# Token rows of the expert dispatch in their own order of channels, loaded into TensorE with a stride of eight columns

## The reference

```python
h2 = modln(x, g_ffn[l], sh_f, sc_f)            # rmsnorm(x, g) * (1 + scale) + shift
# hier_moe: a group by argmax, then the best two experts inside it
xd = zeros((nb * MOE_BLK, d)).at[dest].set(xt[t_s])      # token rows gathered by expert
hid = silu(xb @ w_g[e]) * (xb @ w_u[e])                  # 1024 -> 256, for each expert
yd = hid @ w_d[e]                                        # 256 -> 1024
y = zeros((n, d)).at[t_s].add(yd[dest] * w_s[:, None])
```

## Time and profile before

| | |
|---|---|
| median of three runs | 1427.52 us (1427.38 to 1430.2) |
| the profiled execution, its own time | 1426.45 us |
| its span in the trace | 1424.6 us |
| TensorE busy, mean granted clock | 1215.2 us (85%), 0.945 of full |
| weight loads busy | 919.1 us |
| VectorE / ScalarE busy | 632.7 us / 455.8 us |
| DMA | 356.03 MB, mean 250 GB/s |

### The profile page before, as it was taken

One profiled execution on the slowest core, in us unless ns is written; L12 is line 12 of the kernel. 1 busy time (PEld: TensorE's weight loads), 2 busy tenths in 40 slices (PEclk: granted clock), 3 DMA queues, 4 the chain that ended last, 5 costly groups with the idle time before them and its releaser, 6 DMA issues.

```text
span 1424.6 us, 22233 instructions
## 1 busy us (share of the span) xinstructions
PE 1215.2 (85%) x8870; PEld 919.1 (65%) x8870; DVE 632.7 (44%) x1445; ACT 455.8 (32%) x1043; POOL 138.5 (10%) x175
## 2 busy tenths in 40 slices
PE   5999887999998959999988379998998588888871
PEld 3788754888888647556665278857998464555540
DVE  1545686455445592222221374586767621121213
ACT  2533466433343420001000374265665200010002
POOL 1510000111103230000000200000102000000001
PEclk9999999999999969999999679999999799999996
DMA  9952245323323578999999683267564479999994
GB/s 350 321 168 75 74 152 185 109 89 98 110 89 123 204 260 316 411 419 418 420 422 411 230 243 125 83 205 225 179 186 141 161 323 423 421 420 423 417 422 145
DMA packets 128927, 356.03 MB, mean 250 GB/s; under 512 B 20456, under 2 KB 82144, under 8 KB 104256
## 3 DMA queue, kind: packets, MB, share of 16 engines
q1 hardware_dynamic: 116560, 317.68, 59.5%
q0 software_dynamic: 6528, 18.59, 4.4%
q10 hardware_dynamic: 5744, 18.43, 3.3%
HBM read 332.62 MB, written 22.06 MB: 249 GB/s over the span
## 4 chain that ended last, share of the span: by engine, by line
PE 70%; DMA 12%; DVE 10%; issue 4%; ACT 3%; SPq 0%; POOL 0%; DVEq 0%; ACTq 0%; POOLq 0%
PE banks L924 32%; PE banks L1153 12%; PE banks L1167 7%; DMA ring<-in_w_e_down 6%; PE banks L1145 5%; PE banks L1092 4%; DMA ring<-in_w_e_up 3%; PE banks L1020 2%; PE banks L864 2%; PE banks L1035 2%; PE banks L1005 2%; DMA ring<-in_w_mod 1%; DMA ring<-in_w_in 1%; PE banks L1117 1%; DMA att<-expert_rows,slots_u 1%
## 5 line engine op out<-in xcount | busy, mean ns | idle before, releaser
L1795 DVE TENSOR_TENSOR w_lo<-ring,w_hi 128x256 fp32r<-128x256 f32 x480 | 222.8, 474 | 240.6 <-ACT w_hi L1429 239.4
L1429 ACT ACTIVATE w_hi<-ring 128x256 fp32r<-128x256 f32 x480 | 197.4, 416 | 303.0 <-PE banks L924 253.9
L1153 PE MATMUL banks<-ring,arena 128*64 128x256 f32 x2048 | 233.3, 383 | 33.1 <-issue 16.9
L924 PE MATMUL banks<-h_hi,w_hi 128*128 128x512 f32 (+1 forms) x640 | 221.3, 346 | 7.0 <-DVE h_lo L1726 5.8
L1153 PEld LDWEIGHTS banks<-ring,arena 128*64 128x64 f32 x2048 | 157.0, 137 | 100.3 <-issue 30.6
L924 PE MATMUL banks<-h_lo,w_hi 128*128 128x512 f32 (+1 forms) x640 | 219.8, 343 | 0.0
L924 PE MATMUL banks<-h_hi,w_lo 128*128 128x512 f32 (+1 forms) x640 | 219.6, 343 | 0.0
L1167 PE MATMUL banks<-ring,att 128*64 128x512 f32 x512 | 123.6, 626 | 25.9 <-issue 15.8
L924 PEld LDWEIGHTS banks<-h_hi,w_hi 128*128 128x128 f32 x640 | 122.4, 191 | 23.8 <-ACT arena L1400 5.2
L924 PEld LDWEIGHTS banks<-h_lo,w_hi 128*128 128x128 f32 x640 | 122.5, 191 | 13.7
L924 PEld LDWEIGHTS banks<-h_hi,w_lo 128*128 128x128 f32 x640 | 122.3, 191 | 13.9
(11 more groups left out here) (219 smaller groups left out, 1510.2 us busy)
## 6 DMA issues: line engine op xcount, KB each, us to landing
ring<-in_w_e_gate SPq DMA_DIRECT2D x64, 1024.0 KB, 9.0
ring<-in_w_e_up SPq DMA_DIRECT2D x64, 1024.0 KB, 9.8
ring<-in_w_e_down SPq DMA_DIRECT2D x64, 1024.0 KB, 10.0
ring<-in_w_mod SPq DMA_DIRECT2D x48, 1024.0 KB, 5.2
ring<-in_w_in SPq DMA_DIRECT2D x38, 1024.0 KB, 6.0
expert_rows<-arena ACTq DMA_DIRECT2D x32, 512.0 KB, 8.3
ring<-in_w_o SPq DMA_DIRECT2D x8, 1024.0 KB, 5.1
ring<-in_w_branch SPq DMA_DIRECT2D x8, 640.0 KB, 4.9
```

Source lines behind the costliest of these rows:

```text
L924: ins = mm(out_ap, a, b, start=k == 0 and p_ == 0, stop=k == KD - 1 and p_ == 2)
L1153: ins = mm(banks[e * CAP:(e + 1) * CAP, bank, 0:DE], x[:, k, e * CAP:(e + 1) * CAP], w[:, k * DE:(k + 1) * DE], start=k == 0, stop=k == KD ...
L1429: fn(w_hi[:, u % AHEAD, :, :], chunk(key)[:, q * KU:(q + 1) * KU, :], ACT.Copy).then_inc(w_hi_ready, 1)
L1795: v.tensor_tensor(w_lo[:, u % AHEAD, :, :], chunk(key)[:, q * KU:(q + 1) * KU, :], w_hi[:, u % AHEAD, :, :].bitcast(F32), ALU.subtract).th ...
```

## The change

The row stays in its own order everywhere. Both layers write `htok` plainly, the passes for hi and lo are contiguous in both layers, `turn_h` in layer 1 reads `k::KD`, as layer 0 does already, and `pick_x` loads `h[:, tt, k::KD]` as weights: 128 columns of four bytes, 32 bytes from one to the next. The number of instructions on every engine, their sizes, their order and their waits stay as they were.

```diff
-                        rows = htok[:, tt, k * P:(k + 1) * P] if l else htok[:, tt, k::KD]
+                        rows = htok[:, tt, k::KD]
...
-                        ins = mm(out, h[:, tt, k * P:(k + 1) * P], picked[:, tt, :],
+                        ins = mm(out, h[:, tt, k::KD], picked[:, tt, :],
                                  start=tt == 0 and h is th_hi, stop=tt == QT[l] - 1 and h is th_lo)
...
-                    if l:
-                        ins = fn(htok[:, tt, :].rearrange("p (k s) -> p k s", k=KD)[:, :, 64:P],
-                                 X[:, tt, 512:D].rearrange("p (s k) -> p k s", k=KD), ACT.Copy, scale=r)
-                    else:
-                        ins = fn(htok[:, tt, 512:D], X[:, tt, 512:D], ACT.Copy, scale=r)
-                    ins.then_inc(f_x_act, 1)
+                    fn(htok[:, tt, 512:D], X[:, tt, 512:D], ACT.Copy, scale=r).then_inc(f_x_act, 1)
...
-                        fn(th_hi[:, tt, :].rearrange("p (k s) -> p k s", k=KD),
-                           htok[:, tt, :].rearrange("p (s k) -> p k s", k=KD), ACT.Copy).then_inc(th_hi_ready, 1)
+                        fn(th_hi[:, tt, :], htok[:, tt, :], ACT.Copy).then_inc(th_hi_ready, 1)
...
-                    if l:
-                        ins = v.tensor_scalar(htok[:, tt, :].rearrange("p (k s) -> p k s", k=KD)[:, :, 0:64],
-                                              X[:, tt, 0:512].rearrange("p (s k) -> p k s", k=KD), r, None, ALU.mult)
-                    else:
-                        ins = v.tensor_scalar(htok[:, tt, 0:512], X[:, tt, 0:512], r, None, ALU.mult)
-                    ins.then_inc(f_x_dve, 1)
+                    v.tensor_scalar(htok[:, tt, 0:512], X[:, tt, 0:512], r, None, ALU.mult).then_inc(f_x_dve, 1)
...
-                    h = htok[:, tt, :]
-                    hi, lo = th_hi[:, tt, :], th_lo[:, tt, :]
-                    if l == 0:
-                        h = h.rearrange("p (s k) -> p k s", k=KD)
-                        hi, lo = (x.rearrange("p (k s) -> p k s", k=KD) for x in (hi, lo))
-                    v.tensor_tensor(lo, h, hi.bitcast(F32), ALU.subtract).then_inc(th_lo_ready, 1)
+                    v.tensor_tensor(th_lo[:, tt, :], htok[:, tt, :], th_hi[:, tt, :].bitcast(F32), ALU.subtract)\
+                        .then_inc(th_lo_ready, 1)
```

## The result

The changed kernel takes 1483.31 us, the median of four runs (1479.52 to 1486.01), against 1428.86 us for the kernel before on the same chip (1427.38 to 1433.63): a ratio of 1.037, 95% interval 1.0344 to 1.0396. It is slower, as forecast, but by 54 us and not by 35, and outside the range.

What follows compares the result with a forecast made beforehand. Transfers were taken to bound the expert-stage quads, TensorE close behind. Terms -3.7 + 4.1 + 37 - 4 + 1.7 = +35.1 us on 1426.45 gave 1461.5, forecast 1462 us with the runs' median; range 1423 to 1470.

Steps and rivals of the forecast that it cites:

- the price of a load: Dispatch: the stride halves the load rate, 107 to 213 ns, +107 ns per load at full clock, starts 226 ns apart.
- The savings: Plain row passes: 3.2 us before layer 0's first dispatch, 0.5 us in layer 1, 3.7 us in all.
- The bound of +120: Dispatch: upper bound per load, from L888's 30 ns more for each 32 columns; total then 1469 us.
- L888's pace: Strided loads of `modr` columns: 128, four side by side, in 2.11 us, 66 ns for each four.
- rival 2: Dispatch: load longer by 52 ns as in transposes, pace near 171 ns, +8.6 us, 1436 us; chance 0.14 including values between.
- At half clock a load of 213 ns still fits: Layer 0, quad 0: 26 of 64 matmuls run at half clock and pay nothing for the stride.
- the two quads 0: First quad of each layer, not covered by transfers: +4.1 us in layer 0, +1.7 us in layer 1.
- Layer 0's seven quads: Expert stage: TensorE becomes the bound at 37.7 us a quad, 264 instead of 227.1 us, +37.
- Rival 1: Dispatch: the strided load is hidden, starts stay at 119 ns, only savings remain, 1423.8 us; chance 0.24.
- With the transfers ahead of TensorE these 5 us mostly go: Layer 0's last two pairs, without dispatch: weight waits and a matmul stretch from a clock fall mostly vanish, -4 us.
- Hidden behind the transfers: Layer 1's other quads: 3.4 us added makes 30.9, below the transfers' 32.2 us, so nothing lost.
- layer 1 loses its cover as well: Rival 3: layer 1's quads no longer hidden, up to 24 us more, 1470 to 1486 us; chance 0.02.

Runs made afterwards that it cites:

- the spread order: Changed kernel with each quad's dispatch spread evenly over two pairs, two parts in each, strided loads kept: 1473.59 us against 1429.81 for the kernel before, ratio 1.0297.
- its counterpart: Kernel before with the dispatch spread evenly over two pairs in the same way, loads contiguous: 1426.7 us against 1429.81, ratio 0.9981.

## Why the prediction was right, and where it was wrong

The direction was right, and so was what bounds layer 0 afterwards; the size was not: 53 us by the spans where 35 were forecast. Three steps of the working failed. The largest is the cover in layer 1, put at nothing lost and measured at 11.0 us; then the price of a load, 107 ns taken and 122 measured; then the waits of the last pairs of layer 0, which did not go (-4 forecast, +0.4 measured).

**The savings: right.** L1773 (L1789 before) takes 4.63 us, forecast 4.62; ACT's passes 1057 ns, forecast near 1.06 us; the idle time 10.64 us, forecast 10.6; and it passed whole to TensorE, -3.4 us. The run with contiguous loads agrees with the sum, -4.6 against -3.7 us. The -3.9 us between the stages are more than the row passes of layer 1 (-0.5): there the transposes of L878 met the full clock in the profiled run and the half clock in that of before (16 in 3.65 us, now 2.03), and so did L1117 (4.71, now 3.64 us). That comes to 2.7 us and is a matter of when the clock rises, not of the edit: with the edit too the 16 transposes took 3.65 us in the run with the spread order, and without it 3.07 in its counterpart.

**The price of a load: right in kind, too small.** Forecast +107 ns and starts of 226 ns; measured +122 and 241. The load's own row was to be near 295 ns and is 337: it grew by 149 ns, more than the starts moved apart. The bound of +120, which I worked out from L888's 30 ns for 32 columns and did not take, was right to 2 ns. So was L888's pace: all but the passage of the last, (2.11 - 0.14) / 32 = 62 ns for 32 columns, is 1.9 ns a column and 246 ns for 128. I set it aside as four readers of one memory and took "double", which fits both kinds of strided load loosely and the dispatch's own kind not best. The transposes' loads (192 against 140 ns for the same 128 lines) follow another price, and why is open; leaning on them was the mistake behind rival 2.

**"At half clock a load of 213 ns still fits": wrong in size.** The load costs 241 ns at either level of the clock, so it adds 28 ns to 213 there too. With 28 and 122 ns in place of 0 and 107 the two quads 0 come to +5.4 and +2.4 us; measured +5.0 and +2.0, forecast 4.1 and 1.7.

**Layer 0's seven quads: right.** TensorE became the bound, DMA share 0.89 (under 0.9 forecast), 268.3 us against 264. By the form of my own sum, 30.9 + 64 x 0.122 = 38.7 us a quad, 271 for seven; measured 38.2 and 268.3. Rival 1 fell with the first load.

**"With the transfers ahead of TensorE these 5 us mostly go": wrong.** The last pairs of layer 0 in the changed kernel, as in the earlier trace rows:

```profile
816.41 3.67 PE L1153 MATMUL banks<-ring,arena 128*64 128x256 f32 x32 [0.94 <-issue]
822.24 3.67 PE L1153 MATMUL banks<-ring,arena 128*64 128x256 f32 x32 [2.16 <-issue]
828.25 3.65 PE L1167 MATMUL banks<-ring,att 128*64 128x512 f32 x16 [2.33 <-issue]
```

The waits are there as before. The clock did not fall this time (granted 1.00 from 814 to 823 us, where it was 0.68 from 779.6 to 785.0 before), so the second row takes 3.67 us and not 5.36, but the down product then waits 2.33 us where it waited 0.17: the weights set its time. The ring has six slots, the chunks of one pair; a transfer can be ahead by that and no more, however long TensorE was the bound before. Six chunks of 1 MB take 15 us at 421 GB/s, and a pair without dispatch takes TensorE 11.4 us: it runs dry inside the pair.

**"Hidden behind the transfers" in layer 1: wrong, and the largest miss (11.0 us).** I compared means over a quad, 30.9 against 32.2 us. But the dispatch of a quad stands wholly in one of its two pairs. By the hidden transposes, the pairs of layer 1 took 16.0 and 16.1 us before, and take 20.8 and 12.9 after. In the long one TensorE is behind and gives its slots back late; in the short one TensorE catches up with 11.4 us of work, and 15 us of transfers can't follow, so it waits for weights: 0.4 to 0.6 us in five of the seven short pairs and, more, 1.4 to 2.5 us in five of the seven long ones, for chunks that were issued in the short pair before. Three such pairs of the changed kernel, short, long, short, by windows; then SyncE's and TensorE's timelines around the change from short to long; then the waits of SyncE's queue over the seven quads (us in all, times, longest):

```profile
1244.30:1256.67 12.37, 11.09 (x83) 5.75 (x82) 3.33 (x9) 0.39 (x1) 0.00 (x0) 1.00 0.98 386
1256.67:1278.50 21.83, 19.37 (x117) 14.17 (x116) 3.84 (x8) 2.43 (x3) 0.00 (x0) 1.00 1.01 411
1278.50:1290.90 12.40, 11.10 (x84) 5.77 (x83) 3.33 (x9) 0.39 (x1) 0.00 (x0) 1.00 0.99 394
```

```profile
1252.68 0.81 SPq L668 DMA_DIRECT2D ring<-in_w_e_up  x2
...
1259.02 3.67 PE L1153 MATMUL banks<-ring,arena 128*64 128x256 f32 x32
1265.15 3.67 PE L1153 MATMUL banks<-ring,arena 128*64 128x256 f32 x32 [2.46 <-issue]
```

```profile
SPq L668 <- PE banks L1153: 124.0, 28, 7.8
```

The last row of the timelines stands as "issue", but it is the up weights: the two chunks issued at 1252.68 us, in the short pair, have their last landing at 1265.06 by the trace, 0.09 us before the matmul. In the kernel before SyncE's wait is 106.9 us in 28 times, at most 5.2.

The transfers never stop here, but they run with less in hand. In the kernel before every chunk of this stretch was issued at least 4.3 us before the one ahead of it had landed; in the changed kernel 12 of 81 came later than that, and the rate is 400 GB/s and not 421. That the short lead is what lowers the rate is inferred; that the bunching is the cause is shown by the spread order.

TensorE has 21.5 us more work (192.5 to 214.0), of which its free time took up 10.5 and the window grew by 11.0. The run with the stride in layer 1 alone shows that the loss is made there, and the spread order, which removes the bunching and keeps the loads, brings 224.6 us and 414 GB/s back. It doesn't bring the whole stage back: with its start, layer 1 there is still 7.0 us longer with strided loads than with contiguous ones (248.0 against 241.0 us). The rival "layer 1 loses its cover as well" named the place, with 0.02; its reason, the thin distance of the means, was the weaker one.

Of the 18 us between the forecast (+35.1) and the spans (+53.1), 11.0 are layer 1, 4.4 the last pairs, some 5.4 the price of the load (4.2 in the seven quads, 1.2 in the quads 0), 1.0 the rest of the span, less 3.4 for the clock between the stages and 0.2 at the start.

## What to carry to other kernels

A load of weights whose matmul is just as long has no room: before giving it a stride, count the 16-byte lines that its columns touch, at 1.7 to 1.9 ns each here, and set that against the matmul. Read the price of an operation from the cadence of many of the same kind in the trace, not from the duration of one, and not from another kind that looks alike. And to call work hidden behind a stream, compare it interval by interval with what the buffers hold, never by means over a period longer than the buffering.

## What the runs showed of the hardware

- An ordinary load of float32 weights costs 0.83 ns a column or 1.7 to 1.9 ns per 16-byte line touched, whichever is more (float32 alone was run): starts 119 ns apart contiguous, 120 at stride two, 173 at three, 234 at four, 241 at eight, 222 at sixteen. The 241 ns are the same at half and at full clock.
- The same stride in a transpose costs 52 ns on 140 and keeps starts of 0.11 us (L878). No run here tells why.
- Strided reads of TensorE took little or nothing from the transfers: in the even order layer 1's window was 224.6 us at 414 GB/s with them and 223.8 us at 419 GB/s with contiguous ones.
- Passes of GpSimd over 128x1024 (2.84 to 3.84 us) held three steps of VectorE on 4 elements for 2.6 to 2.8 us, each until the pass ended, and left a reciprocal of the same size alone.
- 1 MB in pieces of 1 KB moved at 365 to 375 GB/s and landed in a median of 11.3 us; in pieces of 8 KB at 414 to 421 GB/s.
